# A two-layer block on one core: delta-rule inverse in 64x64 corner tiles, reordered TensorE passes ahead of the routing

## What is computed

```python
# delta rule, one 64-token chunk, per head
a_low = jnp.where(strict, jnp.einsum('bhnid,bhnjd->bhnij', kb, k) * decay, 0.0)
ia = a_low + jnp.eye(c)
u = triangular_solve(ia, v * beta[..., None])          # unit lower triangular, 64x64
w = triangular_solve(ia, kb * jnp.exp(gc)[..., None])
def step(state, inp):                                  # scan over the 4 chunks
    v_new = u_n - w_n @ state
    o_n = qg_n @ state + qk_n @ v_new
    state = state * gl_n + kd_n.T @ v_new
# end of the first layer
x = x + jnp.einsum('bsd,de->bse', merged, w_out)
h2 = rms_norm(x, ffn_norm_gain)
gate, up = jnp.split(h2 @ w_gate_up, 2, axis=-1)
return x + (jax.nn.silu(gate) * up) @ w_down
# long convolution and filter of the second layer
h = jnp.sin(f_freq[i] * (h @ f_w + f_b))               # three layers
z = irfft(rfft(z) * rfft(k / jnp.sum(jnp.abs(k), axis=0)))
```

## Time and profile before

| | us |
|---|---|
| median of 3 runs | 1153.31 |
| lowest, highest | 1152.03, 1153.62 |
| profiled execution, its own time | 1149.59 |
| its span, first to last instruction | 1147.8 |
| TensorE matmul busy | 983.2 (86%) |
| TensorE weight load busy | 668.0 (58%) |
| VectorE busy | 497.9 (43%) |
| ScalarE busy | 233.7 (20%) |

### The profile page before, as it was taken

The page is one execution under the profiler, slowest core; times in us unless marked ns, Lnnn a source line. Parts: engine busy times, 40 slices in busy tenths (PEclk is TensorE's granted clock), DMA queues, the critical chain, the costliest instruction groups (busy, mean ns, idle before and its releaser), DMA issues.

```text
span 1147.8 us, 18764 instructions
## 1 busy us (share of the span) xinstructions
PE 983.2 (86%) x7876; PEld 668.0 (58%) x7876; DVE 497.9 (43%) x1225; ACT 233.7 (20%) x468; POOL 3.5 (0%) x9
## 2 busy tenths in 40 slices
PE   7999999989899999999999997976776767767676
PEld 5986548856448999954478554543443434433343
DVE  3693926654336556556624756331221222222222
ACT  1015103333110111100311122322222112212222
POOL 0010000000000000000000000000000000000000
PEclk9999999998998999999999998988888888888888
DMA  9545323010422445465400937999999999999996
GB/s 369 210 143 192 130 98 140 1 44 12 183 95 106 167 147 183 185 257 188 178 1 1 383 133 290 412 427 428 428 429 429 429 428 427 429 429 429 428 429 274
DMA packets 25962, 289.55 MB, mean 252 GB/s; under 512 B 2967, under 2 KB 4600, under 8 KB 7992
## 3 DMA queue, kind: packets, MB, share of 16 engines
q1 hardware_dynamic: 25912, 288.83, 61.8%
HBM read 287.77 MB, written 1.05 MB: 252 GB/s over the span
## 4 chain that ended last, share of the span: by engine, by line
PE 59%; DMA 29%; DVE 9%; ACT 1%; issue 1%; SPq 1%; ACTq 0%; DVEq 0%
DMA sb_ring<-w_exp 28%; PE ps L1080 11%; PE ps L399 7%; PE ps L735 6%; PE ps L697 5%; PE ps L1116 5%; PE ps L1170 3%; PE ps L1021 3%; PE ps L990 2%; PE ps L1071 1%; PE ps L1180 1%; PE ps L1154 1%; PE ps L926 1%; PE ps L724 1%; PE ps L937 1%
## 5 line engine op out<-in xcount | busy, mean ns | idle before, releaser
L399 PE MATMUL ps<-sb_ring,sb_own 128*32 128x256 f32 x1984 | 161.5, 493 | 112.7 <-DMA sb_ring<-w_exp 111.8
L399 PEld LDWEIGHTS ps<-sb_ring,sb_own 128*32 128x32 f32 x1984 | 88.8, 140 | 184.6 <-issue 168.4
L2392 DVE TENSOR_TENSOR sb_own<-sb_own,ps 128x128 f32<-128x128 f32 x32 | 9.2, 288 | 321.2 <-ACT sb_own L1608 321.2
L1080 PE MATMUL ps<-sb_nsa,sb_ring 128*128 128x128 f32 x640 | 74.7, 275 | 0.0
L1080 PEld LDWEIGHTS ps<-sb_nsa,sb_ring 128*128 128x128 f32 x640 | 73.1, 192 | 0.0
L419 PE MATMUL ps<-sb_ring,sb_own 128*32 128x256 f32 (+1 forms) x1024 | 61.9, 383 | 7.2 <-DVE sb_own L2392 5.3
L697 PE MATMUL ps<-sb_ring,sb_hT 128*128 128x512 f32 (+1 forms) x160 | 63.7, 556 | 0.5 <-DVE sb_nsa L1816 0.5
L1619 ACT ACTIVATE sb_own<-ps 128x256 f32<-128x256 f32 x32 | 12.3, 383 | 220.3 <-PE ps L399 220.3
L1080 PE MATMUL ps<-sb_hT,sb_ring 128*128 128x128 f32 x480 | 56.9, 275 | 0.0
L1080 PEld LDWEIGHTS ps<-sb_hT,sb_ring 128*128 128x128 f32 x480 | 55.3, 192 | 0.1
L419 PEld LDWEIGHTS ps<-sb_ring,sb_own 128*32 128x32 f32 x1024 | 30.9, 111 | 34.1 <-issue 12.4
(11 more groups left out here) (527 smaller groups left out, 1510.6 us busy)
## 6 DMA issues: line engine op xcount, KB each, us to landing
sb_ring<-w_exp SPq DMA_DIRECT2D x91, 2048.0 KB, 22.2
sb_ring<-w_in SPq DMA_DIRECT2D x13, 2048.0 KB, 7.9
sb_ring<-w_gu SPq DMA_DIRECT2D x11, 2048.0 KB, 7.9
sb_ring<-w_dn SPq DMA_DIRECT2D x10, 1024.0 KB, 6.8
sb_ring<-w_out SPq DMA_DIRECT2D x4, 2048.0 KB, 7.7
sb_ring<-w_branch SPq DMA_DIRECT2D x2, 2048.0 KB, 8.2
sb_ring<-w_in SPq DMA_DIRECT2D x2, 1024.0 KB, 8.9
sb_ring<-cmp_w SPq DMA_DIRECT2D x1, 2048.0 KB, 7.7
```

The lines of the kernel that those rows point to most:

```text
L399: m = pe.matmul(ps[group(j), 2, 0:256], hgT[:, k, :], w[j // 2][k][:, (j % 2) * 256:(j % 2 + 1) * 256], start=(k == 0), stop=(k == KT - 1))
L1080: m = pe.matmul(out[:, i, :], w[:, k, i * P:(i + 1) * P], h[:, k, :], start=start and i == 0 and k == 0, stop=(k == KT // 2 - 1), skip_gro ...
```

## The change

1. Inverse. `aT`, `inv`, `invT`, `off`, `mid` hold only the two diagonal 64x64 corners (64 columns per head), so a unit holds two `off`. Each full matmul becomes two corner matmuls, on partitions 0 to 63 and 64 to 127, both into one bank. VectorE's and ScalarE's operations go over 256 columns instead of 512. The mask of level n + 1 is applied ahead of level n's subtractions. In the last level `inv` is not updated, and its product is left out.
2. u is made per block in corners; w in 64-row tiles, its two chunks in separate banks; copies are split, and `vnew` of chunk 0 waits for the first copy alone.
3. Recurrence. `w state` and `vnew` of the next chunk are made right after the new state, on TensorE and VectorE, ahead of the second attention piece.
4. Projection blocks alternate between bank halves; the first half of block 6 no longer waits for the last sums of block 5. The inverse waits for 8 gate copies instead of 10.
5. Merge. The first filter layer comes ahead of the wait for the merged copies; the first sine ahead of the second block's copies. Rows of x are summed by halves, turned unscaled and multiplied by the gain into `h2_raw`; gate/up's first block runs on these, and its result is scaled afterwards. The squares go to ScalarE. The row scale is widened by two matmuls and applied to all rows behind it. VectorE adds the four magnitudes of the kernel to one, so 4 one-column matmuls are left.
6. The spectra are made in the order 0, 2, 1, 3, and the products go by frequency half, twelve operations over 512 columns.

```diff
@@ TensorE: inverse, u and w, recurrence
                     for h in range(H_GDN):
-                        m = pe.matmul(pair(0)[:, b, h, :], off[:, b, h, :], inv[:, b, h, :], start=True, stop=True)
-
+                        for r in DIAGONAL:
+                            m = pe.matmul(diag(0, b)[r, h, :], off_of(n)[r, b, h, :], inv[r, b, h, :], start=True, stop=True)
...
-                        pe.matmul(pair(2)[:, b, h, :], invT[:, b, h, :], mid[:, b, h, :], start=True, stop=True)
-                        m = pe.matmul(pair(0)[:, b, h, :], mid[:, b, h, :], invT[:, b, h, :], start=True, stop=True)
+                        for r in DIAGONAL:
+                            if n < N_LEVEL - 1:
+                                pe.matmul(diag(2, b)[r, h, :], invT[r, b, h, :], mid[r, b, h, :], start=True, stop=True)
+                            m = pe.matmul(diag(0, b)[r, h, :], mid[r, b, h, :], invT[r, b, h, :], start=True, stop=True)
...
-                    pe.matmul(pair(0)[:, b, h, :], invT[:, b, h, :], vb[:, b, h, :], start=True, stop=True)
-                    m = pe.matmul(pair(2)[:, b, h, :], kbg[:, b, h, :], invT[:, b, h, :], start=True, stop=True)
+                    for r in DIAGONAL:
+                        m = pe.matmul(pair(0)[r, b, h, :], invT[r, b, h, :], vb[r, b, h, :], start=True, stop=True)
+                m.then_inc(sig("uw_made"), 1)
+            for b in range(NB):
+                for h in range(H_GDN):
+                    for n, r in enumerate(DIAGONAL):
+                        m = pe.matmul(by_half(n)[:, b, h, :], kbg[r, b, h, :], invT[r, b, h, :], start=True, stop=True)
...
+                if c < N_CHUNK - 1:
+                    to, rows_to = (c + 1) // 2, slice(CHUNK * ((c + 1) % 2), CHUNK * ((c + 1) % 2) + CHUNK)
+                    pe.wait_ge(sig("state_ready"), c + 1)
+                    for h in heads:
+                        m = pe.matmul(ps[rows_to, 0, h * P:(h + 1) * P], wT[:, to, h, rows_to], state[:, (c + 1) % 2, h, :], start=True, stop=True)
+                    m.then_inc(sig("ws_made"), 1)
                 attention_step(2 * N_LEVEL + 2 * c + 1)
@@ VectorE: inverse and recurrence
             for n in range(N_LEVEL):
                 attention_step(2 * n)
+                for b in range(NB):
+                    if n < N_LEVEL - 1:
+                        level_off(n + 1, b)
                 for b in range(NB):
                     dve.wait_ge(sig("step_made"), NB * n + b + 1)
...
-                    dve.tensor_tensor(inv[:, b], inv[:, b], pair(2 if n else 0)[:, b], ALU.subtract)
-                    dve.tensor_tensor(invT[:, b], invT[:, b], pair(0)[:, b] if n else off[:, b], ALU.subtract).then_inc(sig("inverse_ready"), 1)
...
                     if n < N_LEVEL - 1:
-                        level_off(n + 1, b)
+                        dve.tensor_tensor(inv[:, b], inv[:, b], diag(2 if n else 0, b), ALU.subtract)
+                    dve.tensor_tensor(invT[:, b], invT[:, b], diag(0, b) if n else off_of(0)[:, b], ALU.subtract).then_inc(sig("inverse_ready"), 1)
...
+                    dve.wait_ge(sig("ws_made"), c + 1)
+                    dve.wait_ge(sig("uw_ready"), to + 1)
+                    dve.tensor_tensor(vnew[rows_to, to], uu[rows_to, to], ps[rows_to, 0, :].rearrange("p (h n) -> p h n", h=H_GDN),
+                                      ALU.subtract).then_inc(sig("vnew_ready"), 1)
                 attention_step(2 * N_LEVEL + 2 * c + 1)
@@ TensorE: merge to gate/up
             turn_merged(0)
+            pe.wait_ge(sig("filter_small_loaded"), 48)
+            filter_layer(0)
             pe.wait_ge(sig("mergedT_ready"), since("mergedT_ready", 2))
...
             project_out(0, 0)
+            pe.wait_ge(sig("arg_ready"), since("arg_ready", 1))
             turn_merged(1)
...
+            for half in range(2):
+                turn_x2(0, half)
             project_out(1, 1)
+            turn_x2(1, 0)
...
+                m = pe.matmul(ps[:, 3, ct:ct + 1], kern_abs[:, 0, 0, ct * P:(ct + 1) * P], cols[:, C_ONE:C_ONE + 1], start=True, stop=True)
             m.then_inc(sig("filter_turned"), 1)
...
+            turn_x2(1, 1)
@@ ScalarE
-            plain_out("merge_turned", "mergedT_ready")
-            for n in range(3):
...
+            merged_out(0)
+            filter_sin(0)
+            merged_out(1)
+            filter_sin(1)
+            x2_square(0)
+            filter_sin(2)
...
+            x2_square(1)
+            act.activation(stat[:, 0:NB], stat[:, 0:NB], ACT.Sqrt, bias=cols[:, C_EPS:C_EPS + 1], scale=1.0 / D).then_inc(sig("row_root"), 1)
+            act.wait_ge(sig("x2_widened"), since("x2_widened", 1))
+            act.activation(wide_scale, ps[:, 2, 0:T], ACT.Copy).then_inc(sig("x2_wide_ready"), 1)
@@ VectorE: frequency products
-            dve.wait_ge(sig("zF_ready"), since("zF_ready", 4))
-            re, im = slice(0, 2), slice(2, 4)
...
+            for f in range(2):
+                dve.wait_ge(sig("zF_ready"), since("zF_ready", 2 * f + 2))
+                re, im = f, 2 + f
```

271 lines of the change are left out of this document (153 added, 118 removed).

## The result

| | before | after |
|---|---|---|
| median, us | 1153.46 | 1110.14 |
| lowest, highest (4 runs each) | 1152.03, 1157.65 | 1107.76, 1114.05 |
| profiled execution, its own time | 1149.59 | 1107.76 |
| its span | 1147.8 | 1105.8 |

The ratio is 0.9622, with an interval of 0.9584 to 0.966: the kernel became 43.3 us faster. The prediction had 1125 us (28.5 less than before), with a range of 1115 to 1136: the direction was right, the size too small by 15 us, and the time lies outside the range. In the profiled executions the span fell by 42.0 us against 28.5 forecast.

A forecast was written before the change was run, and what follows sets the result against it. It took TensorE's work to bound the kernel up to 717 us, then expert-weight transfers of fixed length. Terms summed to -28.5 us: 1149.6 became 1121.1, plus 3.7 from profiled execution to median, 1125 us, range 1115 to 1136.

The forecast's parts named there:

- the term for the inverse's matmuls: Inverse: 128 full matmuls at 0.22 us become 240 corner matmuls at 0.0725, 28.2 to 17.4 us, -10.8 us.
- rival 2: Inverse: the clock falls because corners fill a quarter of the array each, one fall per level, 10 us: 1135; chance 0.10.
- the waits of the stage: Delta-rule stage, 171 to 301 us: of 8.5 us of TensorE idle time 2.0 are left, -6.5 us.
- Term (c): Merge to gate/up: the projection behind the wait for the filter's sine takes 7.13 instead of 8.83 us, -1.7 us.
- Rival 1: Inverse: corners don't overlap, a pair costs what the full matmul did; stage gives about 7 instead of 16, 1134; chance 0.14.
- rival 5: Inverse: going from one corner to the other costs a 0.14 us switch each time, slower, 1169 us; chance 0.03.
- Rival 3: Merge's tail stays: half of (b), (d) and (f) is lost, 5.4 us: 1130; chance 0.09.
- (b): Merge to gate/up: TensorE's 2.46 us wait for the sine of filter layer 1 goes with the sine first, -2.5 us.
- (d): Tail between the last projection and gate/up: 10.0 us shrinks to 3.7, -6.3 us.
- (f): Gate/up: less of the 2.5 us lost to a start at the lower clock, -2.0 us, bounds 0 and 2.5.
- Rival 4: Inverse: corners at 0.055 us and no waits left in the levels, -4 and -2 us: 1119; chance 0.10.
- Rival 6: Expert stage hides the gain because its first loads come late: 1153 us; chance 0.01.

The follow-up runs named there:

- e1: Kernel before with the projections' alternating bank halves and shorter block 6 wait alone: 1146.68 us against 1156.68, ratio 0.9924.
- e2: Changed kernel with the old banks and waits of the projections put back: 1117.11 us.
- e3: Changed kernel with corner matmuls reordered so that neighbours share the same corner: 1114.75 us against 1110.77.
- e8: Changed kernel with the product of w and state and the new values back at each chunk's head: 1119.09 us.
- e9: Kernel before with the new order of the recurrence alone: 1143.34 us, ratio 0.9917.
- e13: Changed kernel with the copies of u and w no longer split, TensorE waiting for all before the first chunk: 1119.84 us.
- e6: Kernel before with the reworked merge, filter and norm stretch alone: 1139.85 us against 1155.87, ratio 0.9876.
- e14_grouped_in_place: Changed kernel with old frequency products and each chunk's output products grouped by kind in place: 1107.97 us, ratio to before 0.9586.

## Why the prediction was right in direction and wrong in size

**The step that failed first** is the sentence that the projections ahead of 171 us run gapless but for one wait of 0.5 us. It is false, and the list of waits that it names says so: the longest wait of that list, 4.2 us for VectorE's copies of block 0, is left out there and in the sum. So is the clock behind it, 0.87 from 31.4 to 45 us. Part 4 of the change was therefore priced by the small wait at its end alone. The runs put 6.8 to 7.5 us there (`e1`, `e2`) instead of 0.5, which is 6.3 of the 13.5 us that the sum was short. Another 2.7 belongs to the run: 2.0 by the first projection group, which took 7.14 us in two of 17 profiles, the changed kernel's among them, and 8.56 to 10.20 in the others, and 0.7 by its start.

**The second is the term for the inverse's matmuls.** The mechanism was right, the size was off: -7.8 forecast for matmuls, products and switches, -11.7 in the traces. The corner price was taken from the nearest row as 0.0725; it was 0.067 in the middle products, start of the group included, and 0.0585 in the steps, near the lower bound of 0.055: 96 x 0.067 + 144 x 0.0585 = 14.9 us instead of 17.4. And the 24 switches at 0.14 each (+2.4) aren't to be seen: 28.2 - 14.9 = 13.3 is all that the full-clock profiles have in less busy time (43.20 against 30.05, 13.15). The 0.14 holds for a shape that alternates matmul by matmul, as the grouped outputs confirm (0.86 saved a chunk); a group's start seems to pay once and within its own first row. Against that stands a fall of the clock in one level: 1.3 us of busy time (31.34 against 30.05), 0.6 to 0.9 in the length of the inverse. It is rival 2 in small, and was there for 3.4 us in six of the thirteen profiles with the corner inverse.

**Right in size:** the waits of the stage (-6.5, traces -6.6), but not all where they were expected. The recurrence and the last gate gave 5.9 as worked out; in the inverse, where the early mask was to take most of 2.5 away, 3.0 us of idle time stayed at full clock, and the 0.8 in the table is the low clock's cover. That part is luck. As worked out came the clock in the recurrence of the profiled execution (-1.7); merge to gate/up (-11.1, traces -11.2, alone 13.2 with gate/up against 12.65); the cost of splitting the frequency products (+0.6, traces +0.7); the expert stage, which gave back nothing. Term (c) has the right size, 8.83 to 7.13; its reason isn't confirmed, since the late sine brings back the wait and not the fall behind it.

**The 3.7 us** between the profiled execution and the median were carried over unchanged. They were no constant: by the clocks of the runs and the profile of `e1` they are, at least for the most part, what the low clock costs in a usual execution of before, beyond what its profile showed. After the change the same difference is 2.4 to 3. That part of the gain, 1.5 us at first (3.9 to 2.4), shows in no profile of before.

**The rivals.** Rival 1 and rival 5 fell: corners overlap and neighbours on different corners pay no switch (`e3`). Rival 2 holds for one level. Rival 3 fell: half of (b), (d) and (f) wasn't lost. Rival 4 described the corners best and was held at 0.10, with no row against it but the 0.0725; its other half, no waits left in the levels, didn't hold. Rival 6 fell. Either of the two missed terms alone (6.3 and 3.9 us) would have left the time in the range; both together bring 1125 to its edge, and the 2.7 of the start and the 1.5 of the offset carry it out.

## What to carry to other kernels

Read the whole idle list, the longest wait first, and for each ask whether a part of the diff frees what it waits for; price a part by the largest such wait, not by the last one. After an edit, look at the idle time of the stage and not only at the wait that was to go: another can take its place, as the subtraction's did here. An idle gap of 1.2 to 1.6 us in a stretch of small matmuls can cost 9 to 10 us of half clock behind it, in some executions and not in others; so when one profile shows such a gap with little harm, compare its own time with the spread of the runs before trusting it. Put matmuls of one tile shape in a row and let neighbours use different corners, but move none of them so far ahead that the next link of a dependent chain becomes late.

## What the runs showed of the hardware

- Two 64x64 float32 corner matmuls with 64 moving columns, on the diagonal and into one bank, run side by side at 0.0585 us each; one after the other on the same corner they take 0.117, and a full 128x128 one takes 0.22 (`e3_serial_corners`, `after`, `before`).
- After a gap of 1.2 to 1.6 us between small matmuls, TensorE ran at half its clock for 20 to 34 us in four profiles (`e1`, `e8`, `e9`, `e13`) and for 3.4 us in two (`before`, `e6`); without such a gap the same stretch had full clock in ten of ten.
- The first projection matmuls took between 7.14 and 10.20 us for 32 records with the same code, while the profile's clock column says 1.00. At 7.14 a record follows every 0.22 us from the start; in the fifteen longer ones the first 6 to 14 follow every 0.43 us, up to 13 to 17 us from the start of the span, and the rest every 0.22.
- Four matmuls of one shape and four of another take 2.03 us grouped and 2.89 us alternating (`e14_grouped_in_place`, `after`).
